# Seven half-size products for fifteen projections of the first block and one more of the second, with the weight sums mostly on GpSimd

## What is computed

```
h = rmsnorm(x) * w
z = h @ w_in                      # 6848 columns: hq hf hi hg cq ckv kr gate_a gate_b
o_a = hgrn2(hq, hf, hi) * silu(hg)        # gated linear recurrence over the sequence
o_b = attention(norm(cq) @ w_uq, norm(ckv) @ w_ukv, kr)   # latent attention, 8 heads
y = sigmoid(gate_a) * (o_a @ w_branch_hgrn) + sigmoid(gate_b) * (o_b @ w_branch_mla)
x = x + y @ w_out
x = rmsnorm(x + moe(rmsnorm(x)))  # 64 experts of 1024x512, 1024x512, 512x1024, top 2 of one group
h = rmsnorm(x);  z = h @ w_in_2   # second block: three attentions, three gates
...
```

## Time and profile before

| | |
|---|---|
| median of 3 runs | 1601.19 us (1600.17 to 1602.2) |
| the profiled execution | 1599.81 us, its span 1598.0 us |
| busy over the span | TensorE 1270.6, VectorE 450.5, ScalarE 198.6, GpSimd 0.5 us |
| TensorE clock granted, 0 to 360 us | 1.00 |
| moved by DMA | 506.90 MB, 317 GB/s in the mean |
| first block, expert stream, second block | about 0 to 355, 355 to 1256, 1256 to 1598 us |

### The profile page before, as it was taken

One profiled execution on the slowest core, in us unless ns is written; L12 is line 12 of the kernel. 1 busy time (PEld: TensorE's weight loads), 2 busy tenths in 40 slices (PEclk: granted clock), 3 DMA queues, 4 the chain that ended last, 5 costly groups with the idle time before them and its releaser, 6 DMA issues.

```text
span 1598.0 us, 19255 instructions
## 1 busy us (share of the span) xinstructions
PE 1270.6 (80%) x8526; PEld 776.0 (49%) x8526; DVE 450.5 (28%) x788; ACT 198.6 (12%) x402; POOL 0.5 (0%) x5
## 2 busy tenths in 40 slices
PE   9999999999746856656656665565676999989998
PEld 8656887864313412212212221221221578989985
DVE  3254343232100100100101010010010477698522
ACT  2002023120000000000000000000000211135411
POOL 0000000000000000000000000000000000000000
PEclk9999999999988877877877877887788999999999
DMA  9342256389999999999999999999999654424340
GB/s 387 110 181 107 87 182 256 161 359 402 442 427 437 431 433 430 437 435 433 438 431 436 430 436 431 438 428 440 431 436 426 262 200 159 159 106 164 114 158 27
DMA packets 20558, 506.90 MB, mean 317 GB/s; under 512 B 4240, under 2 KB 4368, under 8 KB 6544
## 3 DMA queue, kind: packets, MB, share of 16 engines
q1 hardware_dynamic: 20208, 505.70, 75.6%
q10 hardware_dynamic: 288, 0.26, 0.0%
HBM read 504.91 MB, written 1.05 MB: 317 GB/s over the span
## 4 chain that ended last, share of the span: by engine, by line
PE 56%; DMA 39%; DVE 3%; issue 1%; ACT 0%; SPq 0%; DVEq 0%; ACTq 0%
DMA ring<-in_experts 37%; PE psP L1218 23%; PE psP L655 9%; PE psP L1270 6%; PE psP L703 4%; PE psP L1268 4%; DMA arena<-in_experts 2%; PE psA L718 2%; PE psP L1371 1%; PE psB L1588 1%; DVE arena L1869 1%; PE psB L1204 1%; PE psA L634 1%; DVE ring L1869 0%; PE psP L1317 0%
## 5 line engine op out<-in xcount | busy, mean ns | idle before, releaser
L655 PE MATMUL psP<-arena 128*32 128x512 f32 x1024 | 145.3, 718 | 130.8 <-DMA arena<-in_experts 130.6
L655 PE MATMUL psP<-ring,arena 128*32 128x512 f32 x1024 | 146.0, 721 | 129.8 <-DMA ring<-in_experts 129.8
L1869 DVE TENSOR_TENSOR X<-X,psA 128x512 f32<-128x512 f32 x66 | 45.3, 688 | 695.5 <-PE psA L718 681.4
L1218 PE MATMUL psP<-arena,ring 128*128 128x256 f32 x896 | 196.1, 379 | 0.0
L1218 PEld LDWEIGHTS psP<-arena,ring 128*128 128x128 f32 x896 | 169.2, 190 | 23.0 <-issue 0.3
L655 PEld LDWEIGHTS psP<-ring,arena 128*32 128x32 f32 x1024 | 37.2, 129 | 235.2 <-issue 231.5
L655 PEld LDWEIGHTS psP<-arena 128*32 128x32 f32 x1024 | 35.1, 129 | 235.4 <-DMA arena<-in_experts 120.2
L1218 PE MATMUL psP<-ring,arena 128*128 128x512 f32 (+2 forms) x368 | 141.9, 543 | 0.0
L1218 PEld LDWEIGHTS psP<-ring,arena 128*128 128x128 f32 x368 | 65.9, 190 | 67.5 <-issue 67.0
L703 PE MATMUL psP<-arena 128*32 128x512 f32 x512 | 66.8, 681 | 26.9 <-DMA arena<-in_experts 25.6
L703 PE MATMUL psP<-ring,arena 128*32 128x512 f32 x512 | 65.9, 667 | 25.8 <-DMA ring<-in_experts 24.5
(11 more groups left out here) (339 smaller groups left out, 1161.9 us busy)
## 6 DMA issues: line engine op xcount, KB each, us to landing
arena<-in_experts SPq DMA_DIRECT2D x7, 4096.0 KB, 21.3
ring<-in_experts SPq DMA_DIRECT2D x7, 4096.0 KB, 22.7
ring<-in_u_gl SPq DMA_DIRECT2D x6, 2048.0 KB, 8.2
ring<-in_u_hq SPq DMA_DIRECT2D x2, 2048.0 KB, 23.5
ring<-in_u_hv SPq DMA_DIRECT2D x2, 2048.0 KB, 12.1
ring<-in_u_hg SPq DMA_DIRECT2D x2, 2048.0 KB, 9.2
ring<-in_u_ga SPq DMA_DIRECT2D x2, 2048.0 KB, 8.6
ring<-in_u_gb SPq DMA_DIRECT2D x2, 2048.0 KB, 8.9
```

The lines of the kernel that those rows point to most:

```text
L655: mm = pe.matmul(z[j * CAP:(j + 1) * CAP, :], x[:, 4 * half + k, j * CAP:(j + 1) * CAP], held[c % 4][:, k // 2, j, (k % 2) * 512:(k % 2 + ...
L1218: mm = pe.matmul(dsts[o], lhs_of(o, k), rhs_of(o, k), start=(k == 0), stop=(k == kc - 1))
L1869: return dve.tensor_tensor(o, a, b, op)
```

## The change

`FAST` gets fifteen projections of the first block in front (`FIRST`) and `dq` of the second. For each group of sources (x, oa, ob, mid) VectorE makes four sums of halves, as the step `halves` with the source's name. GpSimd makes all four weight sums of the units in `FIRST` and of `dq`; for the other fifteen units it makes the first two and VectorE the last two (`sums` is now one step). In the first block GpSimd's order is: the first two sums of unit q, then the fourth of unit q-1, once TensorE has finished the second product of q-1 (which read the quarter that this sum overwrites), then the third of unit q. Buffers are again two deep. The merged result goes straight into the tensor's place; where it had an activation, ACT now does that in place in SBUF. `wa0` and `wa1` are merged into a buffer of their own (in the area of expert chunk 0) and multiplied with their gate after it, `wa1` in a step `gated`, and chunk 0 waits for that. The additions to X after the norm between the blocks move behind the sums of halves. `merge` uses two kept buffers in place of four, and signals `spent`, on which ACT's next copy waits. The load of `wxk` waits for `gb1`.

```diff
+FIRST = ["hq0", "hq1", "hv0", "hv1", "cl", "hg0", "hg1", "ga0", "ga1", "gb0", "gb1", "wa0", "wa1", "wb0", "wb1"]
+FAST = FIRST + ["dq", "dv", "dk", "mv", "mq", "dg", "mk", "mg", "xq", "xg", "gl0", ..., "gl5"]
+BY_TOKENS = {"hv0", "hv1", "cl", "hg0", "hg1", "dq", "dv", "dk", "mv", "mq", "mk"}
...
     def sums(name):
-        p.extend([("sums", (name, 0), ""), ("sums", (name, 1), "")])
+        p.append(("sums", name, ""))
...
-    proj("hf0", "hf1", "hq0", "hq1", "hv0")
+    proj("hf0", "hf1")
+    p.append(("halves", "x", ""))
+    proj("hq0", "hq1", "hv0")
...
-            p.append(("head", ("ga0", 20), ""))
+            p.append(("head", ("ga0", 40), ""))
...
     p.append(("hg_outT", 0, "AB"))
+    p.append(("halves", "oa", ""))
...
     proj("wa1")
+    p.append(("halves", "ob", ""))
+    p.append(("gated", "wa1", ""))
     p.append(("mnorm", 0, ""))
     proj("wb0", "wb1")
...
     proj("mg")
+    sums("xg")
     p.append(("head", ("xq", 16), ""))
...
     p.append(("normal", 6, ""))
-    sums("xg")
     proj("xq")
...
-                if c == 1:
-                    wait_empty(sp, ("proj", "wb1"))
+                if c < 2:
+                    wait_empty(sp, ("proj", ("wa1", "wb1")[c]))
...
         @block.gpsimd
+            def difference(out, a, b):
+                pool.tensor_tensor(out, a, b, ALU.subtract).then_inc(pool_summed, 1)
+            def first_two(arg):
+                w, t1 = unit_ap(arg), sums_of(arg)[0]
+                wait_unit(pool, arg)
+                difference(t1, w[:, 0:4, high], w[:, 0:4, low])
+                pool.wait_ge(pool_summed, POOL_T1[arg])
+                difference(w[:, 0:4, high], w[:, 4:KC, high], w[:, 0:4, high])
+            def third(arg):
+                w, (t1, t2, _) = unit_ap(arg), sums_of(arg)
+                difference(t2, as_sums(w[:, 4:KC, high], t2), as_sums(t1, t2))
+            def fourth(arg):
+                w, (_, t2, t4) = unit_ap(arg), sums_of(arg)
+                pool.wait_ge(pool_summed, POOL_T2[arg])
+                difference(as_sums(t4, t2), as_sums(w[:, 4:KC, low], t2), t2)
+            def fourth_in_place(arg):
+                pool.wait_ge(made, 2 * FAST.index(arg) + 1)
+                fourth(arg)
+            for group in (FIRST[:11], FIRST[11:]):
+                for q, arg in enumerate(group):
+                    if arg == "hq1":
+                        wait_full(pool, ("proj", "hf0"))
+                        wait_empty(pool, ("root_row", "x"))
+                    if arg in ("wa0", "wa1"):
+                        wait_full(pool, ("hg_out", 0))
+                    if arg in last_used:
+                        wait_full(pool, ("proj", last_used[arg]))
+                    first_two(arg)
+                    if q:
+                        fourth_in_place(group[q - 1])
+                    if arg == "gb0":
+                        wait_full(pool, ("cnorm", 0))
+                    third(arg)
+                fourth_in_place(group[-1])
             ...
+            for q, arg in enumerate(FAST[len(FIRST):]):
+                if q >= 2:
+                    wait_full(pool, ("proj", FAST[len(FIRST) + q - 2]))
+                first_two(arg)
+                if arg == "dq":
+                    third(arg)
+                    fourth(arg)
...
                     act.wait_ge(made, 2 * q + 1)
+                    if q:
+                        act.wait_ge(spent, q)
+                    act.activation(kept_for(arg)[0], ps[region_of(key)][:, 0:256], ACT.Copy).then_inc(kept, 1)
+                    if arg[:2] in ("hq", "hg", "ga", "gb"):
+                        act.wait_ge(merged, MERGED[arg])
+                        out_ = rows_of(arg) if arg in BY_TOKENS else feats_of(arg)
+                        act.activation(out_, out_, ACT.Silu if arg[0] == "h" else ACT.Sigmoid).then_inc(empty[r], 1)
...
-            def add_up(arg, part):
+            def add_up(arg):
+                dve.wait_ge(pool_summed, POOL_T1[arg] + 1)
+                tt(t2, w[:, 4:KC, high], t1, ALU.subtract).then_inc(summed, 1)
+                dve.wait_ge(summed, SUMMED[arg])
+                tt(t4, w[:, 4:KC, low], t2, ALU.subtract).then_inc(summed, 1)
```

More of the change, by code:

```diff
@@ L191, in turn @@
             soft(following)
-        if after:
-            p.append(("sums", (after, 0), ""))
         if g == 0:
-            p.append(("head", ("wa0", 3), ""))
+            p.append(("head", ("wa0", 6), ""))
         p.append(("probsT", g, "B"))
@@ L200, in turn @@
         if after:
-            p.append(("sums", (after, 1), ""))
+            sums(after)
         if g == 9:
@@ L226, in plan @@
         if fill[n - 1] == "ch":
-            p.append(("head", ("hg0", 2), ""))
+            p.append(("head", ("hg0", 4), ""))
         p.append(("level", n, "AB" if n <= len(LEVELS) else "A"))
@@ L273, in plan @@
     proj("iq", "ikw")
-    p.append(("head", ("dq", 4), ""))
+    p.append(("head", ("dq", 8), ""))
     p.append(("ropeT", "iq", "AB"))
     p.append(("ropeT", "ik", "AB"))
-    p.append(("halves", "h", ""))
+    p.append(("halves", "mid", ""))
     sums("dv")
@@ L459, in build @@
         relu_s = area(8, 2, 512, off=1024)
-        score = sb("score", [P, 384])
-        dmask = sb("dmask", [P, 384])
         sg = {"mg": area(10, 4, S), "dg": area(10, 4, S, off=1024), "xg": area(11, 4, S)}
         gl = [area(0, KC, S), area(1, KC, S), area(2, KC, S)]
-        h_sums = spare[:, 512:2560].rearrange("p (a k n) -> p a k n", a=4, k=4)
+        four_sums = lambda ap: ap.rearrange("p (a k n) -> p a k n", a=4, k=4)
+        h_sums = {"x": four_sums(spare[:, 0:2048]), "oa": area(4, 4, 4, P), "ob": area(6, 4, 4, P),
+                  "mid": four_sums(spare[:, 512:2560])}
         ring_free = ring[:, SLOTS_2, :]
+        in_fours = lambda ap: ap.rearrange("p (k n) -> p k n", k=4)
+        w_spare = [in_fours(spare[:, 2048 + 1024 * i:3072 + 1024 * i]) for i in range(2)]
+        w_10, w_7, w_8 = ([area(a, 4, 256, off=1024 * i) for i in range(2)] for a in (10, 7, 8))
+        w_apart = [area(8, 4, 256, off=1024), C[:, :, 0:512].rearrange("p t (k n) -> p t k n", k=2)]
+        first_sums = {"hq0": w_spare, "hq1": w_10, "hv0": w_spare, "hv1": w_10, "cl": w_spare, "hg0": w_10,
+                      "hg1": w_spare, "ga0": w_10, "ga1": w_spare, "gb0": w_apart, "gb1": w_spare,
+                      "wa0": w_7, "wa1": w_8, "wb0": w_7, "wb1": w_8}
         w_sums = [[x.rearrange("p (k n) -> p k n", k=4) for x in t] for t in
@@ L530, in build @@
         mid_ready = sem("mid_ready")
-        halved, summed, made, kept, merged = (sem(n) for n in ("halved", "summed", "made", "kept", "merged"))
+        halved, pool_summed, summed, made, kept, merged, spent = (
+            sem(n) for n in ("halved", "pool_summed", "summed", "made", "kept", "merged", "spent"))
         ONE_UP = {"act": (gate_read, selT_copied, y_copied), "dve": (hid_ready, pos_step)}
@@ L1191, in _ @@
         def _(pool):
+            low, high = slice(0, 256), slice(256, 512)
+            def difference(out, a, b):
[16 more added lines that the diff above has]
+                fourth(arg)
+            last_used = {"hv0": "hq0", "hv1": "hq1", "cl": "hv0", "hg0": "hv1", "hg1": "cl", "ga0": "hg0", "ga1": "hg1",
+                         "gb1": "ga1", "wb0": "wa0", "wb1": "wa1"}
+            for group in (FIRST[:11], FIRST[11:]):
+                for q, arg in enumerate(group):
[13 more added lines that the diff above has]
+                fourth_in_place(group[-1])
             pool.wait_ge(rounds_ready, 1)
```

156 lines of the change are left out of this document (102 added, 54 removed).

## The result

The changed kernel takes 1604.36 us in the median of ten runs (1601.79 to 1609.06), the one before 1600.63 beside it (1599.37 to 1602.2): a ratio of 1.0027, 95% interval 1.0019 to 1.0035. It is slower by 4 us, where 1582 had been forecast. The profiled execution took 1605.49 us, its span 1603.7.

The account below looks back on a forecast made before the run. TensorE was taken to bound both dense blocks, the stream of expert weights the middle. 21.35 + 1.65 + 4.5 - 0.4 - 8 = 19.1 us gained gave 1582 us against the 1601.19 median, range 1571 to 1597.

Parts of the forecast that it names:

- The products: First block: fifteen projections by seven half-size products save 1.65 us each token-major, 1.31 feature-major, 21.35 us before the stream.
- the cover: Weight sums, taken at 2.5 us each on GpSimd, finish before TensorE needs them; this fails at 3.4 us per sum.
- The merges: Seven VectorE additions per projection, 2.8 us, fit into idle time and cost nothing, except +0.4 us at `wb1`.
- The stream starts with `wo1`: Fourth expert chunk is issued at the end of `wo1`, so a shorter first block moves all that follows equally.
- The 4.1 us near `xg`: Second block: TensorE's wait for VectorE's merge of `xq` goes, since that merge comes 4.8 us earlier.
- The rival without hindrance: GpSimd and VectorE don't hinder each other: 27.1 us gained, 1574 us; chance 0.22.
- The two engines beside each other: First block: GpSimd and VectorE hindering each other costs between 0 and 16 us; 8 taken.
- The rule of strict turns: Rival: VectorE instructions with two SBUF inputs and GpSimd's SBUF reads wait for each other; 9.1 us gained, 1592; chance 0.22.
- Levels: First-block level periods of 14.9 us instead of 13.5 under turns: 7.4 us; level before `ch` blocked: about 1.5.
- Norm of C: First block, nearly no slack: blocked by one or two GpSimd sums of 2.5 us, about 4 us lost.
- Halves of ob: First block: the sums of ob, behind two of `wb1`'s sums on GpSimd, cost about 3 us.
- The second block's 4.5 us: Two weight sums per projection leave VectorE and `xg`'s sums move ahead: 4.5 of 5.4 us waiting counted as gone.

Follow-up runs that it names:

- e1: Changed kernel with each GpSimd sum replaced by two memsets of its result (no SBUF reads, values not computed): 1574.27 us, ratio 0.9837 to the kernel before.
- e3: Changed kernel with GpSimd waiting for the sums of the halves of ob before `wb1`'s sums: 1598.78 us, ratio 0.9987 to the kernel before.
- e7: Changed kernel with `dq` done by the ordinary product as before, none of its sums on GpSimd: 1598.12 us, ratio 0.9986 to the kernel before.
- e2: Changed kernel with GpSimd waiting for the norm of C to be scaled before `ga0`'s fourth sum: 1594.98 us, ratio 0.9966 to the kernel before.
- e8: Changed kernel with `dq` ordinary and all second-block weight sums on VectorE: 1600.21 us, ratio 1.0 to the kernel before.
- e5: Changed kernel with the waits of e2 and e3, `wb0`'s fourth sum ahead of `wb1`'s first two, `dq` ordinary: 1579.93 us, ratio 0.9876 to the kernel before.

## Why the prediction was wrong

**Right.** The products: token-major projections run in 12.28 us and feature-major ones in 12.5, and in e1 the fourth chunk comes 16.1 us earlier of 21.35; what is missing is 2.0 us of wait at the norm of C, 1.6 of lower clock behind it, 0.4 at `wb1`, and 1.3 in smaller pieces. GpSimd's sum: 2.35 us against 2.5; the text let the cover go "at 3.4 us per sum", but by its own numbers it goes at 2.7 for `hq0` (three sums from 29.5 to 37.5), which 2.35 still meets. TensorE waits for no weight sum in the changed kernel, as costed. The merges cost nothing where VectorE was not held up (masked copies 13.5 us apart in e1, at 119.66 and 133.19, as forecast for the free case). The stream starts with `wo1`: the fourth chunk followed TensorE in both directions, 16 us earlier in e1 and 6 later in the change, and the end of the span with it. The 4.1 us near `xg` disappeared.

**Right by luck.** The rival without hindrance had 1574, and e1 took 1574.3. Its parts do not fit as well: the first block gave 16.1 us where 21 were forecast, and the rest of the run 9.2 where 6.2 were (1241.8 us from the fourth chunk to the end, against 1251.0), and the two errors nearly cancel.

**The step that failed is "The two engines beside each other"**: 8 us taken, 16 as its upper end, some 30 measured (0.9837 against 1.0027). The rule of strict turns stood in the text as a rival; it holds, and even that rival's price, these 16 us and 2 more in the second block, was little over half of the real one. Its parts, against what the traces show:

- *Levels: 7.4 and 1.5 us priced, of which 1.8 lie behind `hg1`. Up to `hg1` that is 7.1 priced and 3.3 measured; the stretch from `ga0` to the attention lost 2.2.* A level period came to 13.8 and 14.2 us (masked copies at 109.43, 123.23 and 137.42), where 14.9 had been laid out. This was the part with the longest working, and too dear.
- *Norm of C: 4 us priced, 11.9 measured.* The working took one or two of GpSimd's sums there. Four in a row meet it, from 140.16 to 153.1 us. The text said of GpSimd's queue that the first two sums of a unit start "when projection q-1 is done"; those of `gb0` have buffers of their own and no such wait, so they follow `ga0`'s fourth and `ga1`'s third without a gap. Three multiplications waited 2.1 us each and the first scaling 1.9, and before them the additions of `hg1`'s merge, held up behind the level before, had pushed the masked copy to 2.4 us behind the end of `hg1`, from 0.7: 9.8 us in all, and less the slack it is the wait of 8.4. Then 2.9 us lost at half clock.
- *Halves of ob: 3 us priced, 9.7 measured (with the 0.4 at `wb1`).* The text put them "behind two of `wb1`'s". GpSimd has `wb0`'s fourth and `wb1`'s third behind these, four sums in a row, and VectorE's group of five additions with the sums of ob in it takes 11.32 us, against 3.76 in e3. Then half clock again.
- *The diagonal between the blocks: not priced at all.* `dq`'s four sums were costed by whether they are ready for `dq`, and its merge by VectorE's idle time. The text did not ask what VectorE does while they run: three additions of 128x2 on which the diagonal hangs, 0.5 us of work with 2.1 us of slack, which lost 5.5. e7 puts the whole price of `dq` at 6.6 us more than its gain.
- *The clock: not priced.* Every wait was costed at its own length. Behind the pauses of 3.3 to 8.4 us comes a stretch at 1.2 GHz, 2 to 3 us more each, 7.8 in all. e2 recovers 10.5 us by removing a wait of 8.4.

**The second block's 4.5 us** were too small. The forecast that the 4.1 us wait would go was right, but e7 gains 6.6 between the fourth chunk and the end, and e8 keeps 4.2 of them without any sum on GpSimd. What the text left out is again the clock, here in its favour: 1.7 us at the lower level behind the wait that went. In the changed kernel `dq`'s losses ate all of it.

Why so much at some places and so little at others follows from one thing. The turn costs VectorE about 2 us per instruction everywhere (2.1 for a multiplication of 128x1024, 1.8 for an addition of 128x512, 1.9 for one of 128x2). In a level period VectorE has 8 us idle, and the loss goes there. At the norm of C there was under a microsecond of slack, and in e3 TensorE still waits 0.2 us at ob, so there was none; nearly all of the loss reached TensorE. At the diagonal there were 2.1 us, and three meetings in a row were more than that. The text had seen the two first of these places, and then priced each by the number of sums that it thought would be there instead of reading GpSimd's order in the code around them.

## What to carry to other kernels

Work that is moved to GpSimd is not priced by GpSimd's idle time, but by which VectorE instructions it meets: in these traces each one with two operands in SBUF, however small, waited for the sum in progress. List the chains of VectorE on which TensorE waits, count the sums that GpSimd's queue can put beside each, and where they outweigh the slack put a wait into GpSimd's queue; here two waits, one exchange of order and leaving `dq` as it was turned 4 us slower into 20 us faster. And cost a new pause of TensorE of 3 us or more at its length and 2 to 3 us on top, as measured here.

## What was not expected of the hardware

- A VectorE addition of 128x2, 0.18 us by itself, took about 2.1 behind a GpSimd sum of 128x1024 (4.19 for two, 1.85 for the third): the price of a meeting is set by the length of the other engine's instruction, not of one's own.
- Instructions with one input wait too: the scaling of 128x384 took 2.29 us beside sums and 1.01 beside memsets, 0.42 alone (e2), while VectorE's multiplications ran undisturbed beside memsets (4.86 in e1). Both agree with the Trainium skill ("SBUF — State Buffer", Who interferes with whom), by which an instruction with two inputs contends with reads alone, and a `tensor_scalar` in a two-port mode with any use of the shared pair. The masked copies and the additions from PSUM kept their 1.3 and 0.4 us throughout.
- After pauses of 8.4, 7.8 and 3.3 us TensorE's granted clock was at 0.50, and it was back at 1.00 within 4 to 8 us of its resuming. Shorter pauses did it too: 0.76 and 0.81 in the two windows of 4 us behind e3's pause of 2.6, 0.73 and 0.84 behind e1's of 2.0. Behind e5's longest pause, 1.4 us at a level, it stayed at 1.00 (108 to 112 us).
